# Seven block products for eight in the up projections of a 128 x 2816 feed forward, with all loops written out

## The reference, cut to what matters

```python
def swiglu(x, w_up, w_down):
    a, b = jnp.split(x @ w_up, 2, axis=-1)       # w_up 1024 x 5632
    return (jax.nn.silu(a) * b) @ w_down         # w_down 2816 x 1024

x = layer_norm(ALPHA * x + 0.5 * swiglu(x, ffn1_w_up, ffn1_w_down), ln1_g, ln1_b)
h, new_buf, S_new = mixer(x, ...)                # projections, short convolution, retention with 4 heads
x = layer_norm(ALPHA * x + h, ln2_g, ln2_b)
x = layer_norm(ALPHA * x + 0.5 * swiglu(x, ffn2_w_up, ffn2_w_down), ln3_g, ln3_b)
```

## Time and profile before

| what | before |
|---|---|
| times of the runs (us) | 1989.85, 1989.98, 1990.23; median 1989.98 |
| span of the profiled execution | 1988.1 us |
| PE busy | 1922.6 us, 97% |
| DVE, ACT, POOL busy | 795.1, 207.6, 936.7 us |
| granted TensorE clock, mean | 0.986 |
| feed forward 1 | from 9.4 us to 470 us |
| boundary, heads, convolution and merge | 470 us to 1475 us |
| boundary, feed forward 2, last norm | 1475 us to 1988 us |

### The profile page before, as it was taken

One profiled execution on the slowest core, in us unless ns is written; L12 is line 12 of the kernel. 1 busy time (PEld: TensorE's weight loads), 2 busy tenths in 40 slices (PEclk: granted clock), 3 DMA queues, 4 the chain that ended last, 5 costly groups with the idle time before them and its releaser, 6 DMA issues.

```text
span 1988.1 us, 29868 instructions
## 1 busy us (share of the span) xinstructions
PE 1922.6 (97%) x11680; PEld 1791.0 (90%) x11680; DVE 795.1 (40%) x1007; ACT 207.6 (10%) x345; POOL 936.7 (47%) x761
## 2 busy tenths in 40 slices
PE   7999999998999999999999999999998999999996
PEld 7999899986889988988989999999978999899985
DVE  5343023325645455355355445323245343023324
ACT  0000000000051051051051000000001100000000
POOL 4555555554433533433433555555553555555552
PEclk9999999998999999999999999999998999999998
DMA  5222222222424525425424322222322222222222
GB/s 209 79 75 74 75 75 74 74 75 64 170 96 149 166 87 171 141 89 171 138 92 169 118 75 75 75 75 75 132 69 69 77 76 75 75 75 74 74 74 74
DMA packets 65518, 196.10 MB, mean 99 GB/s; under 512 B 6176, under 2 KB 8608, under 8 KB 65184
## 3 DMA queue, kind: packets, MB, share of 16 engines
q1 hardware_dynamic: 36288, 132.14, 21.3%
q10 hardware_dynamic: 29152, 62.76, 8.7%
HBM read 170.69 MB, written 24.19 MB: 98 GB/s over the span
## 4 chain that ended last, share of the span: by engine, by line
PE 90%; DVE 6%; issue 3%; ACT 0%; POOL 0%; DMA 0%; DVEq 0%; ACTq 0%; POOLq 0%
PE ps L308 90%; DVE z L899 1%; DVE z L896 1%; DVE ogl L828 1%; DVE xl L828 1%; DVE knh L832 0%; DVE z L861 0%; DVE state L1055 0%; DVE stats L884 0%; DMA xin<-in_x_T 0%; DVE xh L832 0%; DVE z L941 0%; DVE rot L828 0%; DVE ogt L828 0%; PE ps L463 0%
## 5 line engine op out<-in xcount | busy, mean ns | idle before, releaser
L308 PE MATMUL ps<-xh,wl 128*128 128x320 f32 x2560 | 797.8, 312 | 26.8 <-DVE xl L828 18.2
L308 PE MATMUL ps<-xl,wh 128*128 128x320 f32 x2560 | 796.0, 311 | 0.0
L308 PE MATMUL ps<-xh,wh 128*128 128x320 f32 x2560 | 795.6, 311 | 0.0
L280 POOL TENSOR_TENSOR wl<-raw,wh 128x1024 fp32r<-128x1024 f32 x252 | 624.6, 2479 | 21.0
L276 POOL TENSOR_TENSOR idle<-idle 128x8 f32<-128x8 f32 x252 | 55.5, 220 | 1001.9 <-PE ps L308 956.7
L308 PEld LDWEIGHTS ps<-xh,wl 128*128 128x128 f32 x2560 | 485.1, 189 | 31.0 <-DVE xl L828 11.1
L308 PEld LDWEIGHTS ps<-xl,wh 128*128 128x128 f32 x2560 | 485.3, 190 | 0.5
L308 PEld LDWEIGHTS ps<-xh,wh 128*128 128x128 f32 x2560 | 485.1, 189 | 0.0
L278 POOL TENSOR_SCALAR wh<-raw 128x1024 fp32r<-128x1024 f32 x252 | 264.6, 1050 | 0.0
L308 PE MATMUL ps<-wh,hl 128*128 128x512 f32 x440 | 175.7, 399 | 0.0
L308 PE MATMUL ps<-wh,hh 128*128 128x512 f32 x440 | 173.3, 394 | 0.0
(11 more groups left out here) (146 smaller groups left out, 1893.5 us busy)
## 6 DMA issues: line engine op xcount, KB each, us to landing
raw<-in_weights SPq DMA_DIRECT2D x252, 512.0 KB, 3.5
state<-in_state_ret ACTq DMA_DIRECT2D x48, 512.0 KB, 5.7
out_ret_sample<-state ACTq DMA_DIRECT2D x32, 512.0 KB, 3.4
xin<-in_x_T ACTq DMA_DIRECT2D x8, 320.0 KB, 7.0
z_scratch<-z ACTq DMA_DIRECT2D x1, 2560.0 KB, 9.5
z<-z_scratch ACTq DMA_DIRECT2D x1, 2560.0 KB, 9.7
z<-in_x_prompt ACTq DMA_DIRECT2D x1, 2048.0 KB, 15.3
out_ret_prompt<-sp ACTq DMA_DIRECT2D x4, 512.0 KB, 2.7
```

The lines of the kernel that those rows point to most:

```text
L280: pool.tensor_tensor(wl[:, s, :], raw[:, r, :], wh[:, s, :].bitcast(f32), ALU.subtract).then_inc(chunk_split, 1)
L308: ins = nc.tensor.matmul(out, lhs, rhs, start=start, stop=stop)
```

## The change

**Strassen-Winograd on quads.** In each feed forward, tiles 2 to 21 of a and of b (20 of 22) are computed in quads: a block of two column tiles by the two halves of the 1024 input rows, times x cut into 2 x 2 blocks (input rows by tokens, 512 x 320). A plain quad would be 8 block products of 12 matmuls; now it is 7: P1, P6, P7 and P4 into bank x, one into bank y and two into bank w. Each is 4 products of the kind above (12 matmuls of 128x320). There are 20 quads in a feed forward, two for each pair of h tiles (a, then b). Tiles 0 and 1 stay plain units.

**What feeds it.** The weights of a quad are two chunks in `qraw` (4 slots, two quads deep). Four sums of weight blocks are made, S1 and S3 by POOL (`sums`), S2 and S4 by DVE (`second_sum`, `fourth_sum`); the seven operands are rounded by ACT (`quad_hi_part`, into `wqh`) and their low parts made by DVE (`quad_lo_part`, into `wql`). Each slot of `wqh`, `wql` is there once: operand k of quad n + 1 is made once PE is through with operand k of quad n. Four sums of x blocks are made once per feed forward (`x_sums` on DVE into `t`, high parts `th` on ACT, low parts `tl` on DVE). Feed forward 2 has first to add `xh` and `xl` to `xin` again (128x5120).

**What takes the results.** The x bank is a chain: P1, then P6, P7 and P4 are added on top in the same bank, and ACT copies the bank out after each (`chain_copy`; `chain_copied`). PE adds the next product only when the copy is made. DVE makes the four blocks of the result from the copies and the other two banks (`c22_made`, then one addition of 128x640).

**Order.** Groups are now (2, 4, 4, 4, 4, 4): 4 quads, then the down projections of 4 tiles; z is added to 120 times in the feed forwards where it was 40. `LEAD = 1`: one token tile of the down projection is moved ahead of the last two products of a group. POOL and SP have an order written out by hand with sums between the chunk splits. The operation on `idle` is gone. All loops are written out on all engines. In the diff stand POOL's `sums` and `ffn`, PE's `quad`, and DVE's `ffn` and heads.

```diff
+            def sums():
+                n = qk.at
...
+                if n:
+                    pool.wait_ge(quad_ready, made(*divmod(n - 1, QUADS), S12))
+                pool.tensor_tensor(qs[:, 0, :], qraw[:, c0, 512:1024], qraw[:, c1, 512:1024],
+                                   ALU.add).then_inc(pool_sums, 1)
+                if n:
+                    pool.wait_ge(quad_ready, made(*divmod(n - 1, QUADS), S3))
+                pool.tensor_tensor(qs[:, 2, :], qraw[:, c0, 0:512], qraw[:, c0, 512:1024],
+                                   ALU.add).then_inc(pool_sums, 1)
...
+            def ffn(n):
+                split(2)
+                sums()
+                sums()
+                split(4)
+                for g in range(1, len(GROUPS)):
...
+                    sums()
+                    sums()
+                    split(2)
...
+            def quad(n):
...
+                pe.wait_ge(quad_ready, operand(n, S12))
+                product(w, SLOT[S12], n1, True)
+                pe.wait_ge(chain_copied, chained(n, P1))
+                product(x, SLOT[S12] + 1, n2, False).then_inc(chain_full, 1)
+                pe.wait_ge(quad_ready, operand(n, A12))
+                product(y, SLOT[A12], b21, True).then_inc(y_full, 1)
+                pe.wait_ge(chain_copied, chained(n, P6))
+                pe.wait_ge(quad_ready, operand(n, S3))
+                product(x, SLOT[S3], t3, False).then_inc(chain_full, 1)
+                if n % 4 != 3:
+                    first_product(n + 1)
+                else:
+                    led = lead_down()
+                pe.wait_ge(chain_copied, chained(n, P7))
+                pe.wait_ge(quad_ready, operand(n, A22))
+                product(x, SLOT[A22], t4, False).then_inc(chain_full, 1)
+                pe.wait_ge(c22_made, n + 1)
+                pe.wait_ge(quad_ready, operand(n, S4))
+                product(w, SLOT[S4], b22, False).then_inc(psum_full, 3)
...
+            def ffn(k):
+                n = QUADS * k
+                x_sums(k)
+                second_sum(n)
+                fourth_sum(n)
+                plain_tile(0)
+                x_lo_parts(k)
+                for what in range(6):
+                    quad_lo_part(n, what)
+                second_sum(n + 1)
+                fourth_sum(n + 1)
+                plain_tile(1)
...
-            repeat(dve, H, (bk, ad, st, root), (HEAD_BANKS, 24, 48, 2), head, peel=1)
+            for i in range(H):
+                head(i)
...
+            dve.wait_ge(psum_free, bk())
+            step(tt(xin[:, :, :], xh[:, :, :].bitcast(f32), xl[:, :, :].bitcast(f32), ALU.add))
+            after()
+            ffn(1)
```

More of the change, by code:

```diff
@@ L250, in _ @@
         def _(sync):
[L251 to L262, removed]
+            ck, qk = Count(), Count()
@@ new lines, in load, with load_quad @@
+            def load(n):
+                for _ in range(n):
+                    c = ck.at
+                    if c >= NRAW:
+                        sync.wait_ge(chunk_split, c - NRAW + 1)
+                    sync.dma_start(raw[:, c % NRAW, :], a["weights"][c]).then_inc(raw_loaded[c % NRAW], 16)
+                    ck.add()
+            def load_quad(ffn):
+                n, q = qk.at, qk.at - QUADS * ffn
+                for part, what in ((0, S3), (1, A22)):
+                    slot = 2 * (n % NQRAW) + part
+                    if n >= NQRAW:
+                        old = divmod(n - NQRAW, QUADS)
+                        sync.wait_ge(quad_ready, made(*old, what))
+                    sync.dma_start(qraw[:, slot, :], a["quads"][2 * n + part]).then_inc(quad_loaded[slot], 16)
+                qk.add()
@@ L265, in _ @@
+            ffn(0)
+            load(H * HEAD_CHUNKS + 7 * KT)
+            ffn(1)
+            assert (ck.at, qk.at) == (CHUNKS, 2 * QUADS)
         @block.gpsimd
         def _(pool):
[L267 to L281, removed]
@@ L295, in _, with mm @@
             owed = [False]
[L297 to L308, removed]
+            def mm(out, lhs, rhs, start, stop, adds=False):
+                ins = nc.tensor.matmul(out, lhs, rhs, start=start, stop=stop, skip_group_check=adds)
                 if owed[0]:
@@ new lines, in product @@
+            def product(bank_at, slot, x, start):
+                for k in range(4):
+                    last = mm3(ps[:, bank_at, 0:HALF], (cols(k, 128, wqh[:, slot, :]), cols(k, 128, wql[:, slot, :])),
+                               (x[0][:, k, :], x[1][:, k, :]), start and k == 0, k == 3, adds=not start)
+                return last
+            first_half, second_half = slice(0, HALF), slice(HALF, NT)
+            b11 = xh[:, 0:4, first_half], xl[:, 0:4, first_half]
+            b21 = xh[:, 4:8, first_half], xl[:, 4:8, first_half]
@@ L407, in ffn @@
             def ffn(first):
-                for g, tiles in enumerate(GROUPS):
[L409 to L416, removed]
+                if not first:
+                    first_units()
+                for u in range(0 if first else 2, 4):
+                    unit_of_chunk(x_wait=x_piece if first and u == 0 else None)
+                n = 0 if first else QUADS
+                for g, tiles in enumerate(GROUPS):
+                    led = None
+                    if g:
+                        for q in range(4):
+                            led = quad(n)
+                            n += 1
                     h0 = hr.at
@@ L576, in _ @@
             begin_stage()
[L577 to L590, removed]
+            for i in range(H):
+                head(i)
+            for _ in range(3 * KT):
+                unit_of_chunk()
+            for _ in range(KT):
+                unit_of_chunk()
+                unit_of_chunk()
+                pe.wait_ge(conv_ready, KT)
+                unit_of_chunk(zh, zl)
             for half in range(2):
@@ L618, in ln_load, with quad_hi_part @@
                 act.dma_start(lnb[:, :], a[f"ln{k}_b"].to_broadcast([128, D])).then_inc(ln_in, 16)
[L620 to L629, removed]
+            def quad_hi_part(n, what):
+                act.wait_ge(quad_loaded[2 * (n % NQRAW) + (what != A11)], 16 * (n // NQRAW + 1))
+                if what == S12:
+                    act.wait_ge(dve_sums, 2 * n + 1)
+                if what == S3:
+                    act.wait_ge(pool_sums, 2 * n + 2)
+                if what == S4:
+                    act.wait_ge(dve_sums, 2 * n + 2)
+                hi.add()
+                assert hi.at == operand(n, what)
+                copy(quad_slot(wqh, what), quad_source(n, what)).then_inc(quad_hi, 1)
@@ new lines, in chain_copy, with first_copy, window @@
+            def chain_copy(n, product, out, **kw):
+                act.wait_ge(chain_full, chained(n, product))
+                copy(out, ps[:, roles[n][0], 0:HALF], **kw).then_inc(chain_copied, 1)
+            def first_copy(n):
+                chain_copy(n, P1, pu[:, n % 2, 0, :])
+            def window(ffn):
+                for j, t in enumerate((0, 2, 1, 3)):
+                    act.wait_ge(t_summed, 4 * ffn + j + 1)
+                    copy(th[:, t, :], t32[:, t, :]).then_inc(t_hi, 1)
+                b = full(2)
+                result(nc.scalar.activation(two(sig[:, :]), pair(b), ACT.Sigmoid))
+                bk.add(2)
+                for what in range(6):
+                    quad_hi_part(QUADS * ffn, what)
+                act.wait_ge(psum_free, bk())
+                b = full(2)
+                result(nc.scalar.activation(two(sig[:, :]), pair(b), ACT.Sigmoid))
+                bk.add(2 + 2 * TT)
@@ L780, in merge @@
                     bk.add(2)
-            repeat(act, 2, (bk, ad), (24, 4), merge)
+            for i in range(2):
+                merge(i)
             act.wait_ge(z_saved, 16)
@@ L1212, in ffn @@
         for tiles in GROUPS:
-            for f in range(f0, f0 + tiles):
+            for f in range(2 if f0 == 0 else 0):
                 t_unit(up, f * 128)
```

403 lines of the change are left out of this document (331 added, 72 removed).

## The result

| | before | changed |
|---|---|---|
| median of 16 runs each, one chip (us) | 1990.68 | 1996.55 |
| ratio with its 95% interval | | 1.0028 (1.0021 to 1.0036) |
| span of the profiled execution (us) | 1988.1 | 1994.7 |

The kernel is 0.28% slower. The forecast was 2000 us, 0.5% slower. The difference is clear of the measurement, though small, because large terms of both signs nearly cancel.

What follows compares the result with a forecast made beforehand. PE was taken to bound the kernel, busy 97% of the span. Terms -70.4, -11.2, +60.3 and +31.5 sum to +10.2 us on 1988.1, so 1998.3, and 2000 us for the runs shown (0.5% slower); range 1966 to 2026.

Steps and rivals of the forecast that it cites:

- Term 1: Feed forward quads: each goes from 96 to 84 matmuls on PE, 40 quads, -70.4 us.
- Term 2: Mixer heads: writing the loop out removes PE's stand at two loop returns, -11.2 us.
- Term 3: Start of both feed forwards: PE's third unit waits for POOL's split behind quad 1's sums, +60.3 us (50 to 68).
- tail: End of unit 4 in each feed forward: PE stands for `h`, `hh` and `hl` of tile 1, 2.5 us.
- Term 4: Quads 1 and 2 of each group: PE waits because POOL's splits delay DVE, 3.15 us a group, +31.5 us (0 to 50).
- the lock: SBUF port pair: DVE with two SBUF operands and POOL exclude each other for a whole instruction; without it 31 us lower.
- rival "near nothing": Inside the quads: Term 4 costs almost nothing, since waits miss by only 1 to 2 us; 1968.5 us, chance 0.22.
- rival that the clock falls inside the quads: Quad waits merge or exceed 3 us, so each group pays another 2.4 us; 2024 us, chance 0.15.
- rival of loads that cannot follow: Loads of weights or of the longer programs cannot keep up with PE; 2050 us and more, chance 0.04.

Runs made afterwards that it cites:

- heads alone: Kernel before with only the mixer's four heads written out on PE, ACT and DVE: 1979.12 us, ratio 0.9947.
- run with splits first: Changed kernel with the coming down projection's two chunks loaded and split at each group's start, ahead of all sums: 1968.13 us, ratio 0.9888.
- tile's run: Changed kernel with chunks 3 and 4 split before quad 1's sums, and DVE's second plain tile before quad 0's last three low parts: 1971.95 us, ratio 0.9901.
- start experiments: Five runs reordering POOL's or DVE's work at the feed forwards' start, three also with each group's splits first: 1970.30, 1971.95, 1943.30, 1933.96 and 1929.84 us.
- two runs with the second plain tile early: Changed kernel with POOL's start order turned and DVE's second plain tile earlier, 1971.95 us; the same with each group's splits ahead of its sums, 1943.30 us.
- run of POOL's order: Changed kernel with the third and fourth units' chunks split ahead of quad 1's sums at each feed forward's start: 1970.30 us, ratio 0.9900.
- run with three splits first: Second plain tile early and group splits first, plus the first down projection's chunk also split on POOL before quad 1's sums: 1933.96 us, ratio 0.9714.
- last run of the start: Run with three splits first, plus DVE's second plain tile right behind x's low parts and the z wait moved later: 1929.84 us, ratio 0.9694.

## Why the prediction held, term by term

| term | forecast (us) | measured (us) | from |
|---|---|---|---|
| 1, matmuls out | -70.4 | -70.4 | 480 x 0.1466; groups without waits take the sum of their matmuls |
| 2, loops written out | -11.2 | -10.9 to -11.7 alone; -11.4 in the changed kernel | heads alone: three head distances 432.1 against 443.0, medians 1979.12 against 1990.84; in the changed kernel head distances of 143.8, 143.7, 144.1 against the earlier trace rows |
| 3, start of the feed forwards | +60.3 | +63.1 | below |
| 4, waits in the quads | +31.5 | +26.4 | eight groups of 80.17 against 77.26, two with 1.6 |
| sum | +10.2 | +6.6 (spans) | |

**Term 1** was right. It is inferred rather than isolated: no run takes only the matmuls out. The evidence is that a group without waits takes exactly its matmuls' time.

**Term 2** was right, and was shown alone. The stretch from the first norm to the second is another 1.3 us shorter than the heads explain; this was not followed.

**Term 3** was right in its mechanism and 2.8 us too small. In feed forward 1 the third unit began at 55.18, 3.0 later than the 52.2 of the forecast; the step that was short is the wait for z, which ended at 26.5 instead of 23.5. The forecast kept the start of this load as it was before, at 5.86; it is issued at 9.52, since ACT took 8.23 us instead of 4.57 to issue the eight x pieces ahead of it, and it lands after 16.9 us instead of 16.1. The x pieces land after 13.2 us, where it was 7.0. SP's four quad loads beside them are the likely reason; no run varied them.

```profile
9.52 5.83 ACTq L891 DMA_DIRECT2D z<-in_x_sample  x1
```

From there on the chain took 28.7 us, as forecast. The slow clock cost 2.5 (96 matmuls in 16.57 us for 14.08) and the second tile 2.45. Behind this second wait the clock was low once more, which the forecast did not have: the matmuls of the down projection take 0.63 us until 77.3, and the first eight took 3.31 us for 1.87, another 1.4. Together 32.4 us against 28.0. In feed forward 2 the row of DVE's last `xl` of the norm begins at 1507.24 and the third unit at 1543.97, 36.7 us apart, where before they were 1520.16 - 1509.85 = 10.3 us apart; that makes 26.4 us, with clock 2.2 and tail 2.45, less 0.4 that the boundary got shorter: 30.7 against 32.3. The 1.2 us for POOL's sums inside the norm did show in the norm's operation at 1491.48, which took 2.17 us where it took 1.28 before, but the wait ahead of the last `xl` was a microsecond shorter (1.90 for 2.91), so they cost nothing in the end.

**Term 4** was right in place and in kind, and about 5 us too large. The text of the forecast says that without the lock its third term would be nothing; the 31 us that it names are those of this fourth term. The wait in the third quad for ACT's copy, behind the rounding of h, took 1.31 us where 1.9 was forecast, and the wait for the block made by DVE took 1.04 where 1.25 was. A group loses 2.9 us by both. The last group of each feed forward has only the first of the two and loses 1.6, which the forecast had not seen. The run with splits first came out 28.4 us faster, and not 26.4: in its profile the clock stays high behind the wait for the second plain tile (the second matmul of that down projection takes 0.39 us), which gives it the 1.4 us of term 3. The rival "near nothing" is out, and so is the rival that the clock falls inside the quads: it is 1.00 over the whole of a group. The premise of that rival was too simple, though. A stand of 1.97 us ahead of an `xl` left the clock high in the kernel before; in the changed kernel the same stand, at 1509.78, is followed by matmuls at the low clock from 1510.97 to 1514.17.

```profile
209.54:289.71 80.17, 77.81 (x457) 71.78 (x457) 51.10 (x57) 26.98 (x45) 28.33 (x16) 1.00 0.24 80
...
1479.00:1544.00 65.00, 27.38 (x150) 24.95 (x148) 56.40 (x59) 16.36 (x23) 22.10 (x10) 0.69 0.07 24
```

These are two stretches: a group in the steady course and the boundary to feed forward 2 (busy us of PE, PEld, DVE, ACT, POOL, then the clock, the DMA share and GB/s). In the first DVE is busy for 51 of 80 us and nobody is short of time on average. In the second PE works 27 of 65 us and DVE 56.

**The balance of the spans** closes: -70.4 - 11.4 + 63.1 + 26.4 = +7.7, and 1.3 less for the rest of the middle is +6.4, where the spans are 6.6 apart. The forecast's sum was +10.2. That it came so near is in part luck: term 3 was 2.8 us too small and term 4 was 5.1 us too large.

The rival of loads that cannot follow is out as well: quads read through the four slots of `qraw`, and PE never waited for a DMA. What I had not asked is who else stands behind the sums on POOL. That cost nothing in the forecast, where the third unit hid the fifth chunk, but it spoiled the expectation of the tile's run. The expectations of the start experiments were all too good (by 9, 23, 21, 3 and 8 us). For the two runs with the second plain tile early, most of the miss is the overlooked fifth chunk; in the other three, work that was moved ahead on one of DVE and POOL landed beside the other's (the x sums in the run of POOL's order, the four `tl` of feed forward 2 in the run with three splits first, 7.90 us for 5.69, and those of feed forward 1 in the last).

## What to carry to other kernels

Taking matmuls out of a kernel that PE bounds is worth what it promises only if the operands' preparation has no in-order queue in front of PE: follow, for each queue that the new work enters, everything that was behind that place already. Here one operation's place on POOL (a split behind two sums that wait) made PE stand for 23.3 and 25.4 us, and turning the order of the same work made a loss of 0.3% a gain of 3.1%. Two engines that shut each other out of a port want their long operations put where the other has none to do, not merely enough time on average.

## What the runs showed of the hardware that I had not expected

The forecast had DVE and POOL take turns, but POOL does not always get its turn. In the rows of the quads the two alternate, but at 46.36 POOL's sum of 512 took 3.36 us, where it needs 1.26: DVE's four low parts from 46.10 to 48.6 went through without a gap, each in 0.69 us. In the last run of the start, a sum at 51.59 went through in 1.57 us between two low parts. What decides is open.

A wait of one length does not always leave the same clock. The 2.45 us ahead of the second tile's down projection were followed by the low clock in feed forward 1 of the changed kernel (0.63 us for a matmul of 128x512 behind 74.19), but not in its feed forward 2 (0.39 us from 1563.03 on), nor in feed forward 1 of the run with splits first. In feed forward 1 of the changed kernel PE had come back from the 23.25 us wait at 55.18, and from the low clock at 60.14; in its feed forward 2 it had as long a wait behind it, so that alone does not tell the two apart.

A return of a hardware loop costs PE about 5.5 us when its body is one head. When it is four units of 48 matmuls, as in the feed forwards of the kernel before, PE's list of waits shows none for it. The Trainium skill, page "Runtime: NRT & Kernel Launch", section "Instruction fetch mechanics", says that a taken branch to a target outside what is fetched makes the engine wait for the fetch; the run with the heads written out agrees with it, and no run here varied the size of the body.
